# Feed-forward of a streaming encoder on one core: groups of four output tiles, 512-column matmuls and the left-over sums placed by VectorE and ScalarE

## What is computed

```python
def conv_ffn(h, buf, w_up, w_gate, conv_w, conv_b, w_down):
    up = h @ w_up
    gate = h @ w_gate
    ext = jnp.concatenate([buf.astype(gate.dtype), gate], 1)
    act = jax.nn.gelu(causal_dwconv(ext, conv_w, L) + conv_b)
    return (act * up) @ w_down, ext[:, -(FFN_CONV - 1):]
# per layer: x = x + mixer(rms_norm(x)); x = x + conv_ffn(rms_norm(x)); at the end rms_norm(x)
```

## Time and profile before

| | us |
|---|---|
| Median of 3 runs | 2826.82 (2825.56 to 2827.31) |
| The profiled execution | 2826.28 |
| Its span, first to last instruction | 2824.5 |
| PE busy | 2805.3 (99%) |
| VectorE busy | 1555.3 (55%) |
| ScalarE busy | 1032.5 (37%) |
| GpSimd busy | 123.6 (4%) |
| DMA, mean share of 16 engines | 45% |
| Chain that ended last: PE at L463 | 95% |

### The profile page before, as it was taken

How to read it: one execution, slowest core, us unless ns; L and a number is a source line. 1 busy time by engine, 2 the same in 40 slices (tenths; PEclk the granted TensorE clock), 3 DMA queues, 4 the chain that set the end, 5 groups by cost and what they waited for, 6 DMA issues and landing times.

```text
span 2824.5 us, 49617 instructions
## 1 busy us (share of the span) xinstructions
PE 2805.3 (99%) x19055; PEld 2791.5 (99%) x19055; DVE 1555.3 (55%) x2178; ACT 1032.5 (37%) x1135; POOL 123.6 (4%) x136
## 2 busy tenths in 40 slices
PE   9999999999999999999999999999999999999998
PEld 8999999999999999999999999999999999999998
DVE  7666645554355544555666666455554455535554
ACT  5443333333333333333444444443333333333333
POOL 0000021000000000002200000220000000000012
PEclk9999999999999999999999999999999999999999
DMA  6444344444444444444444444444444444444443
GB/s 237 145 145 137 129 149 149 151 148 151 151 149 144 155 150 149 142 155 149 144 146 151 136 143 142 154 147 151 148 150 149 149 149 149 149 149 149 149 149 114
DMA packets 120784, 420.26 MB, mean 149 GB/s; under 512 B 13688, under 2 KB 19840, under 8 KB 120576
## 3 DMA queue, kind: packets, MB, share of 16 engines
q1 hardware_dynamic: 120128, 418.45, 44.7%
q10 hardware_dynamic: 576, 0.66, 0.1%
HBM read 412.92 MB, written 6.14 MB: 148 GB/s over the span
## 4 chain that ended last, share of the span: by engine, by line
PE 98%; DVE 1%; DMA 0%; ACT 0%; issue 0%; DVEq 0%; ACTq 0%
PE gb L463 95%; PE ab L469 3%; PE ab L482 1%; DMA x<-in_x 0%; DVE w_lo L1097 0%; PE ab L663 0%; DVE work L1731 0%; DVE work L1225 0%; DVE rt L1727 0%; DVE work L1189 0%; ACT w_hi L785 0%; DVE a_lo L1104 0%; DVEq L140 0%; ACT work L862 0%; ACTq L850 0%
## 5 line engine op out<-in xcount | busy, mean ns | idle before, releaser
L1097 DVE TENSOR_TENSOR w_lo<-raw,w_hi 128x1024 fp32r<-128x1024 f32 x767 | 943.4, 1230 | 1175.5 <-ACT w_hi L785 1173.5
L785 ACT ACTIVATE w_hi<-raw 128x1024 fp32r<-128x1024 f32 x769 | 814.5, 1060 | 1653.8 <-PE gb L463 1651.4
L463 PE MATMUL gb<-a_hi,w_hi 128*128 128x320 f32 x4216 | 1311.1, 311 | 0.5 <-DVE w_lo L1097 0.3
L463 PE MATMUL gb<-a_hi,w_lo 128*128 128x320 f32 x4216 | 1302.8, 309 | 0.0
L463 PE MATMUL gb<-a_lo,w_hi 128*128 128x320 f32 x4216 | 1302.7, 309 | 0.0
L463 PEld LDWEIGHTS gb<-a_hi,w_hi 128*128 128x128 f32 x4216 | 791.6, 188 | 2.2 <-DVE w_lo L1097 0.6
L463 PEld LDWEIGHTS gb<-a_lo,w_hi 128*128 128x128 f32 x4216 | 791.6, 188 | 1.2
L463 PEld LDWEIGHTS gb<-a_hi,w_lo 128*128 128x128 f32 x4216 | 791.3, 188 | 0.0
L463 PE MATMUL gb<-b_hi,w_hi 128*128 128x320 f32 x1920 | 593.7, 309 | 0.0
L463 PE MATMUL gb<-b_hi,w_lo 128*128 128x320 f32 x1920 | 593.3, 309 | 0.0
L463 PE MATMUL gb<-b_lo,w_hi 128*128 128x320 f32 x1920 | 593.3, 309 | 0.0
(11 more groups left out here) (182 smaller groups left out, 804.6 us busy)
## 6 DMA issues: line engine op xcount, KB each, us to landing
raw<-in_weights SPq DMA_DIRECT2D x769, 512.0 KB, 3.3
out_y<-work SPq DMA_DIRECT2D x4, 640.0 KB, 3.0
out_c<-work SPq DMA_DIRECT2D x8, 257.0 KB, 5.6
x<-in_x SPq DMA_DIRECT2D x3, 640.0 KB, 7.8
work<-m_scratch SPq DMA_DIRECT2D x8, 192.0 KB, 4.9
work<-in_ret_tables SPq DMA_DIRECT2D x8, 160.0 KB, 3.3
work<-in_ml_state SPq DMA_DIRECT2D x8, 128.5 KB, 5.2
work<-in_w_pool SPq DMA_DIRECT2D x1, 1024.0 KB, 8.5
```

The source lines that it names most:

```text
L463: last = nc.tensor.matmul(bank(b, m), w[:, at:at + P], v[:, t:t + T], start=kg == k == n == 0, stop=kg == groups - 1 and k == UK - 1 and n ...
L785: nc.scalar.activation(w_hi[:, at:at + UW], raw[:, at:at + UW], ACT.Copy).then_inc(hi_ready, 1)
L1097: V.tensor_tensor(w_lo[:, at:at + UW], raw[:, at:at + UW], w_hi[:, at:at + UW].bitcast(F32), ALU.subtract).then_inc(lo_ready, 1)
```

## The change

**Groups and quads.** Gate pair and up pair of the same hidden tiles now form a group of four output tiles (banks 0 to 3), and in the down projection two neighbouring output pairs do. A quad is the two units (one of each pair) for the same 4 input tiles. Where the units lie in HBM is turned round to match. hi and lo of a tile now lie side by side in one array (`a`, `b`), 640 columns per tile.

**Matmuls.** `wide_quad` issues for each weight tile one matmul of `w_hi` on 512 columns: the 320 of hi and the first 192 of lo. They go to different columns of the bank (0 to 319 and 320 to 511). `w_lo` on hi stays a matmul of 320. The last 128 columns of lo are left: `left_of` takes them as the stationary operand and `w_hi` of both units (512 columns) as the moving one, so that the left-over sums come out with tokens on the partitions, in one bank of `ab` for all four output tiles. They run one quad ahead of the rest. `hi_ready` is now waited for by PE as well.

**Putting the parts together.** `turn_left` transposes the left bank in 32x32 blocks, in one VectorE instruction; `place_left` moves the 16 blocks to their places with 16 ScalarE copies (32 partitions by 128 elements), in two lots of eight, between splits. VectorE adds the 192 columns from each bank (`lows_of`) and the placed 128: `ffn_gate`, `ffn_up`, `add_wide_to_x` and `left_to_x`.

**Order.** Both pairs of a group now end in its last quad: pair 0 with the last quad's eight `w_lo` matmuls ahead of the eight of pair 1, with which the group ends. In the VectorE program `ffn_gate` (pair 0), a split, `ffn_up` (pair 1), two splits and `ffn_conv` follow one another; in ScalarE's, the gelu of the group before stands between the splits of the group's units 4 and 5 (counted from 0). The very last quad of the kernel keeps the pairs apart (`apart`). In all other stages `unit` stays as it was but for the new places of hi and lo.

The core of the diff (the down projection of the short block, the first group and the new reading of `a` and `b` elsewhere follow the same lines):

```diff
+        a, b = sb("a", KT * 2 * T, F32R), sb("b", KT * 2 * T, F32R)
...
+            def left_of(u, q, quads, act):
+
+                for k in range(UK):
+                    t = (q * UK + k) * 2 * T + T + WIDE_LO
+                    w = w_hi[:, u.slot * UW:(u.slot + 2) * UW].rearrange("p (u k c) -> p u k c", u=2, k=UK)
+                    last = nc.tensor.matmul(left_bank, act[:, t:t + P], w[:, :, k, :], start=q == k == 0,
+                                            stop=q == quads - 1 and k == UK - 1)
+                return last
+
+            def wide_quad(u, q, quads, act, taken, group, apart=False, f_all=None):
+
+                final = q == quads - 1
+                if q == 0:
+                    pe.wait_ge(hi_ready, u.number(2))
+                    pe.wait_ge(left_turned, group)
+                    left_of(u, 0, quads, act)
+
+                def next_left():
+                    if final:
+                        return
+                    pe.wait_ge(hi_ready, u.number(4))
+                    last = left_of(u.plus(2), q + 1, quads, act)
+                    if q + 1 == quads - 1:
+                        last.then_inc(left_summed, 1)
+
+                def high_weights(p):
+                    if q == 0:
+                        pe.wait_ge(pair_taken, taken + p)
+                    for m in range(UM):
+                        for k in range(UK):
+                            at, t = u.plus(p).slot * UW + (k * UM + m) * P, (q * UK + k) * 2 * T
+                            nc.tensor.matmul(gb[:, 2 * p + m, :], w_hi[:, at:at + P], act[:, t:t + 512],
+                                             start=q == k == 0, stop=False)
+
+                def low_weights(p):
+                    pe.wait_ge(lo_ready, u.number(p + 1))
+                    for m in range(UM):
+                        for k in range(UK):
+                            at, t = u.plus(p).slot * UW + (k * UM + m) * P, (q * UK + k) * 2 * T
+                            last = nc.tensor.matmul(bank(p, m), w_lo[:, at:at + P], act[:, t:t + T],
+                                                    start=False, stop=final and k == UK - 1)
+                    last.then_inc(unit_used, 1)
+
+                if apart and final:
+                    for p in range(2):
+                        high_weights(p)
+                        low_weights(p)
+                    return
+                for p in range(2):
+                    high_weights(p)
+                if f_all is None:
+                    next_left()
+                for p in range(2):
+                    low_weights(p)
+                if f_all is not None:
+                    pe.wait_ge(f_ready, f_all)
+                    next_left()
...
+            def place_left(group, half):
+
+                act.wait_ge(left_turned, group + 1)
+                if half == 0:
+                    act.wait_ge(left_added, group)
+                for tokens in (2 * half, 2 * half + 1):
+                    for feats in range(4):
+                        last = nc.scalar.activation(left_t_blocks[feats * 32:(feats + 1) * 32, :, tokens, :],
+                                                    left_blocks[tokens * 32:(tokens + 1) * 32, :, feats, :], ACT.Copy)
+                last.then_inc(left_placed, 1)
...
                     with act.Fori(0, k // 2 - 1) as i:
                         for j in range(8):
                             split(Unit(u0 + AHEAD + 8 + j, i, 8))
                             if j == 1:
+                                ffn_gelu(i + g)
+                            if j == 2:
                                 ffn_upper(i + g, i * 2)
-                            if j == 6:
-                                ffn_gelu(i + (g + 1))
-                    groups = k // UK
-                    final = b == len(BLOCKS) - 1
-                    for kg in range(groups):
-                        split(Unit(down_u + AHEAD + kg))
-                        if kg == 0:
...
+            def turn_left(group):
+
+                dve.wait_ge(left_summed, group + 1)
+                dve.wait_ge(left_placed, group * 2)
+                V.transpose(left, ab[:, 1, :]).then_inc(left_turned, 1)
+
+            def left_to_x(group, p):
+
+                dve.wait_ge(left_placed, group * 2 + 2)
+                at = x[:, bass.ds(p * 2 * T, 4 * T)].rearrange("p (m t) -> p m t", m=4)[:, :, WIDE_LO:T]
+                V.tensor_tensor(at, at, left_t.rearrange("p (m t) -> p m t", m=4), ALU.add).then_inc(left_added, 1)
+                dve.wait_ge(left_added, group + 1)
+
+            def add_wide_to_x(p, b, units, taken):
+
+                own()
+                used(units)
+                step.inc(V.tensor_tensor(two(tiles(x, p * 2)), banks(b), two(tiles(x, p * 2)), ALU.add))
+                own()
+                V.tensor_tensor(two(tiles(x, p * 2))[:, :, 0:WIDE_LO], lows_of(b),
+                                two(tiles(x, p * 2))[:, :, 0:WIDE_LO], ALU.add).then_inc(pair_taken, 1)
+                dve.wait_ge(pair_taken, taken)
...
+                used(units)
+                r = both(rt[:])
+                V.tensor_tensor(two(low_gate)[:, :, 0:WIDE_LO], lows_of(0), r[:, :, 0:WIDE_LO], ALU.mult)
+                V.tensor_tensor(ext[:, :, 2:2 + SEQ], banks(0)[:, :, 0:SEQ], r[:, :, 0:SEQ], ALU.mult)
+                V.tensor_tensor(ext[:, :, s0:GE], banks(0)[:, :, SEQ:T], r[:, :, SEQ:T], ALU.mult)\
                     .then_inc(pair_taken, 1)
-                dve.wait_ge(pair_taken, taken)
+                dve.wait_ge(left_placed, group * 2 + 2)
+                V.tensor_tensor(low_both.rearrange("p (m t) -> p m t", m=4)[:, :, WIDE_LO:T],
+                                left_t.rearrange("p (m t) -> p m t", m=4),
+                                rt[:, WIDE_LO:T].unsqueeze(1).to_broadcast([P, 4, P]), ALU.mult)\
...
+            def ffn_up(units, taken):
 
                 used(units)
-                V.tensor_tensor(two(up), banks(1), both(rt[:]), ALU.mult).then_inc(pair_taken, 1)
+                r, ext, s0 = both(rt[:]), two(g_ext, GE), 2 + SEQ + 2
+                V.tensor_tensor(two(low_up)[:, :, 0:WIDE_LO], lows_of(1), r[:, :, 0:WIDE_LO], ALU.mult)
+                V.tensor_tensor(two(up), banks(1), r, ALU.mult).then_inc(pair_taken, 1)
                 dve.wait_ge(pair_taken, taken)
+                lo = two(low_gate)
+                V.tensor_tensor(ext[:, :, 2:2 + SEQ], ext[:, :, 2:2 + SEQ], lo[:, :, 0:SEQ], ALU.add)
+                V.tensor_tensor(ext[:, :, s0:GE], ext[:, :, s0:GE], lo[:, :, SEQ:T], ALU.add).then_inc(gate_scaled, 1)
+                step.inc(V.tensor_tensor(up, up, low_up, ALU.add))
+
...
+                    with counted(dve, k // 2 - 1, [(step, 3)]) as i:
+                        for j in range(8):
+                            if j == 0:
+                                ffn_up(i * 8 + (u0 + 8), i * 2 + (p0 + 2))
+                                split(Unit(u0 + AHEAD + 7, i, 8))
+                            if j == 7:
+                                ffn_gate(layer, i * 2 + (f + 2), i * 8 + (u0 + 15), i + (group + 1))
+                                split(Unit(u0 + AHEAD + 14, i, 8))
+                                continue
+                            if j == 3:
+                                ffn_lower(i + g, i * 2)
+                            if j == 5:
+                                turn_left(i + (group + 1))
+                            if j != 6:
+                                split(Unit(u0 + AHEAD + 8 + j, i, 8))
+                            if j == 0:
+                                ffn_conv(layer, i * 2 + f, i + g)
+                            if j == 1:
+                                ffn_product(i + g)
+                    group += k // 2
+                    quads = k // UK
...
+                        with counted(dve, 3, [(step, 2)]) as i:
+                            for j in range(8):
+                                if j == 0:
+                                    add_wide_to_x(i * 2 + 1, 1, i * 8 + (down_u + 8), i * 2 + (down_p + 2))
+                                    split(Unit(down_u + AHEAD + 7, i, 8))
+                                if j == 7:
+                                    left_to_x(i + (group + 1), i * 2 + 2)
+                                    add_wide_to_x(i * 2 + 2, 0, i * 8 + (down_u + 15), i * 2 + (down_p + 3))
+                                    split(Unit(down_u + AHEAD + 14, i, 8))
+                                    continue
+                                if j == 5:
+                                    turn_left(i + (group + 1))
+                                if j != 6:
+                                    split(Unit(down_u + AHEAD + 8 + j, i, 8))
```

More of the change, by code:

```diff
@@ L26 @@
 UW = UK * UM * P
+WIDE_LO = 512 - T
 AHEAD = RING - 1
@@ L558, in first_unit @@
                     for m in range(UM):
-                        at, t = (k * UM + m) * P, k * T
-                        for n, (w, v) in enumerate(((w_hi, a_hi), (w_hi, a_lo), (w_lo, a_hi))):
```

(34 more changed lines are left out.)

318 lines of the change are left out of this document (182 added, 136 removed).

## The result

The changed kernel takes **2864.03 us** (median of 4 runs, 2863.74 to 2866.38) against 2826.88 (4 runs, 2825.56 to 2827.31): ratio 1.0134, 95% interval 1.0116 to 1.0152. It is slower by 37 us, where the prediction had 15: the direction and the wide range (2803 to 2870) held; the size did not, and 2864 lies above the forecast's own range (2833 to 2856). The profiled execution took 2863.74 with a span of 2861.9.

The account below looks back on a forecast made before the run. PE, busy 2805.3 of 2824.5 us, was taken as the bound. Matmuls -42.2, bank waits +49.5, second wait +6 and tail +2 sum to +15, giving 2842 us; own range 2833 to 2856, 8 in 10 2803 to 2870.

Parts of the forecast that it names:

- The matmuls: Feed-forward quads: 48 matmuls become 36 for the same columns, saving 0.160 us a quad over 264 quads, -42.2 us.
- H: Start-to-start time of a 512-column matmul, taken as 213.3 + 13.3 = 226.7 ns, the overhead being per matmul.
- Both rivals on it: Small overhead: 512 columns take 215.3 ns, 2805 us, chance 0.20. Overhead per column: 234.7 ns, 2872 us, chance 0.14.
- The bank wait behind a gate/up group: At 44 boundaries PE waits 0.74 us each for VectorE to read pair 1's banks.
- a sign of being wrong: PE's waits standing at the start of a group for the left sums, or PE showing no waits; no size.
- The second wait: Left sums issued in quad 1: PE waits 0.13 us for unit 5's w_hi, behind convolution and gelu; x 44, +6 us.
- The bank wait behind a down group: At 22 down-projection boundaries PE waits 0.77 us each for pair 1, as VectorE makes two adds per pair.
- The step on the copies: ScalarE's sixteen placing copies take 3.2 us, the last split ready two us before PE asks; costs nothing.
- placing is dear: Rival: ScalarE copies at 0.47 or more make PE wait 1.06 instead of 0.74; +21, 2863 us, chance 0.06.
- The tail: Kernel's end: output pair 6 ends in the last quad, so the root starts at 4.6 instead of 2.7; +2 us.

Follow-up runs that it names:

- experiment 4: Changed kernel, gate/up loops: VectorE reads pair 1's up sums first, and ScalarE's second lot of copies comes two units later; 2863.01 us, ratio 1.0129 to the kernel before.
- experiment 7: experiment 5 plus, in down groups, adds ahead of the copies' wait and later second copies; gelu's order in first down groups too; 2811.72 us, ratio 0.9949.
- Experiment 1: Changed kernel with two of the sixteen placing copies left, the other fourteen left out of the computation; 2844.25 us, ratio 1.0062 to the kernel before.
- experiment 5: experiment 4 plus ScalarE making w_hi of unit five ahead of the gelu in the gate/up loops; 2835.25 us, ratio 1.0029 to the kernel before.
- the third edit: ScalarE's w_hi of unit five ahead of the gelu, gate/up loops; alone on the changed kernel 2865.33 us, on top of experiment 4 2835.25 us.
- three single edits: Each alone on the changed kernel, gate/up loops: pair 1 read first, 2862.6 us; second copies two units later, 2864.59; w_hi of unit five before gelu, 2865.33.

## Why the prediction was half right

- **The matmuls (-42.2): right.** In the timeline of experiment 4 four left-over matmuls and the sixteen of `w_lo` behind them follow without a wait: 2301.49 to 2302.39 is 0.90 for four of 512 columns, 0.225 each, 2302.39 to 2304.73 is 2.34 for sixteen of 320, 0.146 each. Over all matmuls of the groups the median distance is 0.227 and 0.147; 0.227 is the H that was chosen. Both rivals on it fall (0.216 and 0.235). The saving could be cashed: experiment 7 is 15 us below the kernel before. The rule of the Trainium skill that the prediction cited (TensorE: Matmul & The Clock Gate, Back-to-back issue gap) does not agree with the trace: it gives 0.136 at 320 columns and 0.216 at 512.
- **The bank wait behind a gate/up group (0.74 each, 32.6): right.** Experiment 1 shows 0.77. In the changed kernel it was 0.44 because 0.33 of it were already spent at the group's start. That start wait stands at a group's first left-over sums (`PEld ab L498 <- issue: 14.9, 51`), which the prediction had named as a sign of being wrong: its split was to be two us early and was late. That the 44 boundaries together came out near the forecast (37.3 for 32.6 and 6) is partly luck, since the 6 did not come and the 3.5 us of slipping were in no term.
- **The second wait (+6): right in its mechanism, absent from this kernel.** The chain over convolution, gelu and unit five's w_hi was worked out to T + 12.29, 0.13 behind PE; it was ready 0.18 to 0.20 before PE. With the first two waits gone (experiment 4) it costs 0.7 a boundary (0.61 and the 0.11 that follows a stop), and 28 us went with it in experiment 5.
- **The bank wait behind a down group (0.77 each, 17): the step that failed.** It started VectorE's adds at T - 0.96, with no term for waiting on the placed columns. The step on the copies ("What lies beside") had placed the last one at T - 3.0 from "16 x (0.29 - 0.09) = 3.2 us" and "two us before PE asks for it. So nothing". The 0.09 of overlap was read from other instructions. These copies had none: 0.32 from start to start, 5.1 us for sixteen. The last one ends at T - 1.0, L1241 follows it, and the adds start 0.96 late (2211.01 where PE's last low product would have let them start at 2210.05). Measured 24.1 for the 16 boundaries of the 16-tile blocks, 1.51 each, and 6.7 for the other six: 30.8 where the forecast had 17. Each 12-tile block adds 2.3 us in its first down group, where the chain from the turn over the copies to w_hi has only 5.8 us (2769.97 to 2775.75) instead of 8.0 (2202.96 to 2211.01); this place was not looked at. With two copies instead of sixteen (experiment 1) the 22 boundaries cost 16.5 and the last quads nothing: the forecast's 17 was right but for the copies. Of the 22 missing us the down boundaries make 18.5.
- **The rival "placing is dear"** said 2863 and had 0.06. It had the right cause, but the number is luck: it wanted copies of 0.47 and set the wait at PE's own w_hi (+21 us over the boundaries). The copies took 0.32, and experiment 1 finds nothing to gain behind the gate/up groups. The cost sat behind VectorE's add.
- **The tail (+2): 3.7.** The root (L882) starts at 2849.68, 6.4 us after T = 2843.30, the slot's end of the feed-forward's last matmul; 4.6 was forecast and 2.7 was the time before. GpSimd's squares of pair 6 took the 3.8 of the forecast (2843.38 to 2847.15) but began at T and not 1.2 before it, since L1241 had to wait for the copies there too; the passes of the norm were slower by 0.6:

```profile
2843.38 0.72 POOL L454 TENSOR_TENSOR sq_one<-x 128x320 f32 x1 [9.00 <-DVE x L1250]
...
2846.03 0.87 POOL L456 TENSOR_TENSOR sq_sum<-sq_sum,sq_one 128x320 f32<-128x320 f32 x1
...
2846.96 0.19 POOL L467 COPY sq_one<-sq_sum 128x1 f32<-128x1 f32 x1
2847.20 0.30 PEld L552 LDWEIGHTS ab<-sq_sum,con 128*128 128x128 f32 x2 [4.00 <-POOL sq_one L467]
...
2847.84 1.80 PE L552 MATMUL ab<-work,con 128*128 128x320 f32 x4
2849.68 0.53 ACT L882 ACTIVATE std<-ab,con 128x320 f32<-128x320 f32 x1 [2.40 <-PE ab L552]
```

Not tried: the order of the 12-tile blocks' down groups (4.7 us in the last quads and 6.7 at their other boundaries in the changed kernel), the tail, and the third edit with only one of the other two.

## What to carry to other kernels

A slack is a sum of its own, and has to be worked out with the start-to-start time of the very shape that fills it: sixteen small copies here took 5.1 us instead of 3.2, because the sum had subtracted an overlap that was measured on other instructions, and those 1.9 us were the cover of everything behind them. Where a group has several waits of about the same length, each can hide the next: here three single edits gave 1.4 us or nothing, and so did the one pair that was tried; the 28 us came with the third edit. So an experiment without effect does not clear its suspect: look where the wait went, and remove that one too. And put the instruction that frees a bank ahead of whatever on its engine can wait for a third engine.

## What the runs showed of the hardware

- ScalarE's copies of 32 partitions x 128 elements take 0.308 us and follow at 0.32 from start to start, while its 128 x 1024 splits take 1.06 and follow at 0.95. Being small is not the reason: in the kernel before, a ScalarE instruction of 128 x 64 elements that takes 0.35 is followed at 0.25, an overlap of 0.1. A split with one of these copies behind it does not overlap either (2206.37 + 1.06 against 2207.45). The copies differ in spanning 32 partitions, in moving data from one set of partitions to another and in their strides; which of these it is stays open.

```profile
1503.50 0.35 ACT L990 ACTIVATE work<-work 128x64 f32<-128x64 f32 x1 [2.23 <-DVE work L1559]
1503.75 0.62 ACT L992 ACTIVATE work<-work 128x512 f32<-128x512 f32 x1
```

- The overhead of an fp32r matmul at full clock is per instruction: 146.7 ns at 320 columns and 226.7 at 512 are 13.3 ns over 320 / 2.4 and 512 / 2.4, both times.
- After PE has stood still, the first matmul is followed by the second at 335 ns instead of 227, whatever its kind (left-over or wide). So a wait costs about 0.1 us more than its length; in experiment 4 this is 0.11 behind each 0.61.
- The last two of the six norm passes at the end of the kernel followed at 0.53 us instead of the 0.27 of the earlier trace rows. PE had been idle for 3.7 us, and during the passes TensorE's granted clock fell from 1.00 to 0.50 (the 1.2 GHz level); the window over the slow ones has 0.56 (columns as in the earlier trace rows). The six passes reach from 2847.20 to 2849.64, 2.4 us instead of the forecast's 1.8.

```profile
2847.20:2848.20 1.00, 1.00 (x4) 0.76 (x5) 0.00 (x0) 0.08 (x1) 0.00 (x0) 1.00 0.00 0
2848.20:2849.70 1.50, 1.45 (x4) 0.43 (x2) 0.00 (x0) 0.01 (x1) 0.00 (x0) 0.56 0.00 0
```
